# A halved first slab, slab splits between the angles, a staggered odd layer and shorter waits in the state steps of a two-block network on one core

## The reference

```
for l in range(DEPTH):
    hn = rms_norm(h, attn_norm[l])
    proj = hn @ w_in[l]
    ...
def rope(x, positions):
    inv = ROPE_BASE ** (-jnp.arange(0, d, 2, dtype=jnp.float32) / d)
    ang = positions.astype(jnp.float32)[..., None] * inv
    cos, sin = jnp.cos(ang), jnp.sin(ang)
...
def step(state, inp):                      # RWKV-7, done in chunks of 64 tokens
    sa = jnp.einsum('bhvk,bhk->bhv', state, -kkt)
    state = (state * wt[:, :, None, :] + sa[..., None] * (kkt * at)[:, :, None, :]
             + vt[..., None] * kt[:, :, None, :])
...
def odd_layer(x, norm_pre, ...):
    h = rmsnorm(x, norm_pre)
    proj = h @ w_in                        # q, k, v, r, lr
```

## Time and profile before

| | |
|---|---|
| median of 3 runs | 2118.84 us (2118.39 to 2123.34) |
| profiled execution | 2119.92 us, span 2118.1 us |
| PE busy | 2010.8 us, 95% |
| DVE busy | 1124.9 us, 53% |
| ACT busy | 824.2 us, 39% |
| POOL busy | 92.5 us, 4% |
| first matmul | 14.10 us |

### The profile page before, as it was taken

The page is one execution under the profiler, slowest core; times in us unless marked ns, Lnnn a source line. Parts: engine busy times, 40 slices in busy tenths (PEclk is TensorE's granted clock), DMA queues, the critical chain, the costliest instruction groups (busy, mean ns, idle before and its releaser), DMA issues.

```text
span 2118.1 us, 29241 instructions
## 1 busy us (share of the span) xinstructions
PE 2010.8 (95%) x12552; PEld 1616.5 (76%) x12552; DVE 1124.9 (53%) x1566; ACT 824.2 (39%) x1160; POOL 92.5 (4%) x61
## 2 busy tenths in 40 slices
PE   6998799999999999888899999999999999889997
PEld 4875487888888887647688888887778777679886
DVE  7456755543344545567554434447667673543373
ACT  4246533322222323664332222235464653324362
POOL 4010120000000000103000000000000000100000
PEclk9999999999999999989999999999999999999999
DMA  5310011222322322100032232223222222222111
GB/s 210 110 60 23 2 43 60 100 87 82 119 100 69 121 90 82 40 1 23 27 108 90 86 121 88 86 95 119 100 80 99 81 80 99 80 71 79 60 51 40
DMA packets 26192, 167.35 MB, mean 79 GB/s; under 512 B 2896, under 2 KB 3152, under 8 KB 10192
## 3 DMA queue, kind: packets, MB, share of 16 engines
q1 hardware_dynamic: 26064, 165.48, 22.4%
HBM read 163.38 MB, written 2.10 MB: 78 GB/s over the span
## 4 chain that ended last, share of the span: by engine, by line
PE 87%; DVE 9%; ACT 3%; issue 1%; DMA 0%; DVEq 0%; SPq 0%; ACTq 0%
PE bank L670 25%; PE bank L671 24%; PE bank L672 24%; PE bank L696 5%; PE bank L901 3%; DVE ring_low L1920 2%; ACT ring_high L1397 1%; PE bank L802 1%; DVE bank L2155 1%; PE bank L915 1%; DVE arena L2168 1%; PE bank L1268 1%; PE bank L1287 1%; DVE arena L2219 1%; PE bank L889 0%
## 5 line engine op out<-in xcount | busy, mean ns | idle before, releaser
L670 PE MATMUL bank<-arena_split,ring_high 128*128 128x512 f32 x2188 | 869.3, 397 | 48.6 <-DVE ring_low L1920 37.1
L671 PE MATMUL bank<-arena_split,ring_high 128*128 128x512 f32 x2188 | 857.7, 392 | 0.0
L672 PE MATMUL bank<-arena_split,ring_low 128*128 128x512 f32 x2188 | 857.2, 392 | 0.0
L670 PEld LDWEIGHTS bank<-arena_split,ring_high 128*128 128x128 f32 x2188 | 414.6, 190 | 149.2 <-DVE ring_low L1920 27.5
L671 PEld LDWEIGHTS bank<-arena_split,ring_high 128*128 128x128 f32 x2188 | 414.6, 189 | 89.1 <-issue 4.5
L672 PEld LDWEIGHTS bank<-arena_split,ring_low 128*128 128x128 f32 x2188 | 414.3, 189 | 87.2
L1920 DVE TENSOR_TENSOR ring_low<-ring,ring_high 128x2048 fp32r<-128x2048 f32 (+3 forms) x161 | 344.4, 2140 | 176.6 <-ACT ring_high L1397 176.0
L1397 ACT ACTIVATE ring_high<-ring 128x2048 fp32r<-128x2048 f32 (+3 forms) x161 | 284.6, 1769 | 382.6 <-PE bank L672 379.8
L1415 ACT ACTIVATE arena<-bank 128x512 f32<-128x512 f32 x72 | 43.1, 598 | 291.5 <-DVE bank L1901 291.5
L1901 DVE TENSOR_TENSOR bank<-bank,rstd 128x512 f32<-128x512 f32 x72 | 50.3, 698 | 121.5 <-PE bank L672 121.5
L1366 ACT ACTIVATE arena<-bank 128x512 f32<-128x512 f32 (+1 forms) x73 | 42.3, 594 | 137.5 <-PE bank L672 62.6
(11 more groups left out here) (343 smaller groups left out, 1829.2 us busy)
## 6 DMA issues: line engine op xcount, KB each, us to landing
ring<-slabs_in SPq DMA_DIRECT2D x122, 1024.0 KB, 4.8
ring<-slabs_in SPq DMA_DIRECT2D x32, 704.0 KB, 4.1
con<-con_in SPq DMA_DIRECT2D x1, 2208.0 KB, 12.0
h<-x_in SPq DMA_DIRECT2D x4, 512.0 KB, 9.1
out<-arena SPq DMA_DIRECT2D x8, 256.0 KB, 2.0
ring<-slabs_in SPq DMA_DIRECT2D x3, 512.0 KB, 3.4
ring<-slabs_in SPq DMA_DIRECT2D x2, 768.0 KB, 4.4
arena<-gates_in SPq DMA_DIRECT2D x1, 1536.0 KB, 9.8
```

Of the source, the lines that this page charges most:

```text
L670: pe.matmul(out, weight[0], right[0], start=start, stop=False)
L671: pe.matmul(out, weight[0], right[1], start=False, stop=False)
L672: return pe.matmul(out, weight[1], right[0], start=False, stop=stop)
```

## The change

Six edits, all to the order of work and its waits. The arithmetic stays.

First, the slab `in0_r` comes in two transfers of half its columns, the transfers of x between them, and each half is split by itself; PE's first group waits for the first half alone. ACT loads its table at once, and POOL starts its squares when the first slab is split. Second, the split of `in0_v` goes into the middle of the first angle, and the split of `in0_lo_mq0` behind the angles; the norm's sum moves from the middle of `in0_k` into the middle of `in0_v`. Third, in the odd layer each tile's step has three products, two for `qk` 0 and 1 and one for 2 or 3; the other eight follow when all tiles are there, and `slab_group` of `odd_qk0` names group `qk` 1. The splits of `odd_qk2` and `odd_qk3` stand ahead of the norm's root on ACT and DVE, the norm's sum stands between `qk` 4 and 5, and POOL waits for all eight squares. Fourth, the copies that signalled `transition_ready` and `state_ready` go; PE waits for the addition itself. Fifth, on DVE `in0_mq12` is split behind two evictions of banks instead of six. Sixth, the squares of the last head are summed one product step earlier.

```
@@ tensor engine
             def norm_sum(tag):
+                pe.wait_ge(ones_loaded, 16)
                 pe.wait_ge(squares_summed, cnt.next(squares_summed))
...
-                pe.wait_ge(transition_ready, cnt.next(transition_ready))
+                for n in range(2):
+                    pe.wait_ge(*taken(("G", l, n)))
                 for c in range(1, NC - 1):
...
-                    pe.wait_ge(state_ready, cnt.next(state_ready))
                     bk = group(("st", l, c), "dve")
+                    if c == 1:
+                        pe.wait_ge(state_ready, cnt.next(state_ready))
+                    else:
+                        pe.wait_ge(*taken(("st", l, c - 1)))
...
-                pe.wait_ge(state_ready, cnt.next(state_ready))
+                pe.wait_ge(*taken(("st", l, NC - 2)))
...
-                pair(f"in{l}_r", [("pa", l, 0), ("pa", l, 1)], ["dve"] * 2, parts_step, (lambda: norm_sum(("attn", l))) if l else None)
-                pair(f"in{l}_k", [("pa", l, 2), ("pa", l, 3)], ["dve"] * 2, None, None if l else (lambda: norm_sum(("attn", l))))
-                pair(f"in{l}_v", [("pa", l, 4), ("pa", l, 5)], ["dve"] * 2)
+                if l:
+                    pair(f"in{l}_r", [("pa", l, 0), ("pa", l, 1)], ["dve"] * 2, parts_step, lambda: norm_sum(("attn", l)))
+                else:
+                    first = ring_high[:, 0, :], ring_low[:, 0, :]
+                    pe.wait_ge(first_half_split, 1)
+                    split_gemm(("pa", l, 0), "dve", split_tiles(first, 0, DT), hn_parts, parts_step)
+                    split_gemm(("pa", l, 1), "dve", split_tiles(split_slab(f"in{l}_r"), DT * P, DT), hn_parts)
+                pair(f"in{l}_k", [("pa", l, 2), ("pa", l, 3)], ["dve"] * 2)
+                pair(f"in{l}_v", [("pa", l, 4), ("pa", l, 5)], ["dve"] * 2, None, None if l else (lambda: norm_sum(("attn", l))))
...
+            later = [(n, k) for k in range(DT) for n in (2, 3)]
             for k in range(DT):
                 parts_step(k)
-                for n, (bk, w) in enumerate(held):
-                    mm = product(bk[:, :], w[k], hn_parts[k], k == 0, k == DT - 1)
-                    if k == DT - 1:
-                        mm.then_inc(psum_ready, 1)
+                for n in range(2):
+                    odd_product(n, k)
+                odd_product(*later.pop(0))
+            for n, k in later:
+                odd_product(n, k)
             for n in range(2):
-                slab_group[slab_index[f"odd_qk{n}"]] = len(order) - 1
...
+                slab_group[slab_index[f"odd_qk{n}"]] = book["qk", 2 * n + 1][0]
...
+            pair("odd_qk2", [("qk", 4), ("qk", 5)], ["dve"] * 2, None, odd_norm_sum)
+            pair("odd_qk3", [("qk", 6), ("qk", 7)], ["dve"] * 2)
...
-                    if n == 0 and k == 1:
+                    if n == 0 and k == 0:
                         gla_squares(3, last_squares)
@@ scalar engine
+            act.preload_act_table_set(ROOTS)
             act.wait_ge(epsilon_ready, cnt.next(epsilon_ready, 5))
...
                         if m == 1:
-                            prepare(f"in{l}_r", 1)
+                            act.wait_ge(first_half_loaded, 16)
+                            f(ring_high[:, 0, FIRST_HALF], ring[:, 0, FIRST_HALF], ACT.Copy).then_inc(cnt.up(first_half_high), 1)
+                    act.wait_ge(slab_loaded[0], 16)
+                    f(ring_high[:, 0, SECOND_HALF], ring[:, 0, SECOND_HALF], ACT.Copy).then_inc(cnt.up(slab_high_ready), 1)
...
                 if l == 0:
+                    prepare(f"in{l}_k")
...
-                    prepare(f"in{l}_k")
+                    prepare(f"in{l}_v")
...
+            prepare("odd_qk2")
             inverse_root(("ss", "odd"), rstd[:, :], D)
-            for m in range(4):
-                prepare(f"odd_qk{m}")
+            prepare("odd_qk3")
@@ vector engine
                         ts(turns, turns, MAGIC, None, SUB).then_inc(cnt.up(dve_done), 1)
-                        dve.wait_ge(cnt.sem, cnt.value)
+                        turned_down = cnt.value
+                        if n == 0:
+                            prepare(f"in{l}_k")
+                        dve.wait_ge(dve_done, turned_down)
...
-                    prepare(f"in{l}_k")
+                    prepare(f"in{l}_v")
...
+                    if m == 2 and l == 0:
+                        prepare(f"in{l}_lo_mq0")
...
                        ADD).then_inc(cnt.up(dve_released), 1)
-                    dve.wait_ge(cnt.sem, cnt.value)
-                    cp(stat[:, 0, 0:1], stat[:, 1, 0:1]).then_inc(cnt.up(state_ready), 1)
...
             post_norm("even_post", "even_post", residual_ready, lambda m: f"even_out{m}", 16, "odd_pre")
+            prepare("odd_qk2")
@@ gpsimd
+            pool.wait_ge(slab_split, 1)
...
+            pool.wait_ge(residual_square_ready, DT)
             for m in range(DT):
-                pool.wait_ge(residual_square_ready, m + 1)
@@ sync
-                sp.dma_start(ring[:, n % SLOTS, 0:cols], src).then_inc(slab_loaded[n % SLOTS], 16)
+                if n == 0:
+                    sp.dma_start(ring[:, 0, FIRST_HALF], src[:, FIRST_HALF]).then_inc(first_half_loaded, 16)
+                    for m in range(1, 4):
+                        sp.dma_start(h[:, 2 * m:2 * m + 2, :], x_in[:, 2 * m:2 * m + 2, :]).then_inc(x_loaded[m], 16)
+                    sp.dma_start(ring[:, 0, SECOND_HALF], src[:, SECOND_HALF]).then_inc(slab_loaded[0], 16)
```

More of the change, by code:

```diff
@@ L403, in A @@
             return arena[:, t:t + n, :]
+        FIRST_HALF = slice(0, DT * P)
+        SECOND_HALF = slice(DT * P, 2 * DT * P)
         def R(t):
@@ L427, in two_blocks @@
         slab_high_ready, slab_split = sem("slab_high_ready"), sem("slab_split")
+        first_half_loaded = sem("first_half_loaded")
+        first_half_high, first_half_split = sem("first_half_high"), sem("first_half_split")
         high_ready, parts_ready = sem("high_ready"), sem("parts_ready")
@@ L473, in two_blocks @@
         end_diagonal_ready = sem("end_diagonal_ready")
-        transition_ready = sem("transition_ready")
         state_ready = sem("state_ready")
@@ L1170, in _, with odd_product, odd_norm_sum @@
                 held.append((group(("qk", n), "dve"), w))
+            def odd_product(n, k):
+                bk, w = held[n]
+                mm = product(bk[:, :], w[k], hn_parts[k], k == 0, k == DT - 1)
+                if k == DT - 1:
+                    mm.then_inc(psum_ready, 1)
+            later = [(n, k) for k in range(DT) for n in (2, 3)]
             for k in range(DT):
                 parts_step(k)
-                for n, (bk, w) in enumerate(held):
-                    mm = product(bk[:, :], w[k], hn_parts[k], k == 0, k == DT - 1)
-                    if k == DT - 1:
-                        mm.then_inc(psum_ready, 1)
-            for n in range(2):
-                slab_group[slab_index[f"odd_qk{n}"]] = len(order) - 1
-            pe.wait_ge(odd_squares_summed, 1)
-            gemm(("ss", "odd"), "act", rows, [cst("ones")], [A(8)[:, 0, :]])
-            for n in range(2, 4):
-                pair(f"odd_qk{n}", [("qk", 2 * n), ("qk", 2 * n + 1)], ["dve"] * 2)
+                for n in range(2):
[3 more added lines that the diff above has]
+                odd_product(n, k)
+            for n in range(2):
+                slab_group[slab_index[f"odd_qk{n}"]] = book["qk", 2 * n + 1][0]
+            def odd_norm_sum():
+                pe.wait_ge(odd_squares_summed, 1)
+                gemm(("ss", "odd"), "act", rows, [cst("ones")], [A(8)[:, 0, :]])
+            pair("odd_qk2", [("qk", 4), ("qk", 5)], ["dve"] * 2, None, odd_norm_sum)
+            pair("odd_qk3", [("qk", 6), ("qk", 7)], ["dve"] * 2)
             split_gemm("lr", "dve", split_tiles(split_slab("odd_lr"), 0, DT), hn_parts)
@@ L1425, in _ @@
                         if m == 1:
-                            prepare(f"in{l}_r", 1)
+                            act.wait_ge(first_half_loaded, 16)
+                            f(ring_high[:, 0, FIRST_HALF], ring[:, 0, FIRST_HALF], ACT.Copy).then_inc(cnt.up(first_half_high), 1)
+                    act.wait_ge(slab_loaded[0], 16)
+                    f(ring_high[:, 0, SECOND_HALF], ring[:, 0, SECOND_HALF], ACT.Copy).then_inc(cnt.up(slab_high_ready), 1)
+                    splits.append(f"in{l}_r")
                 prepare(f"in{l}_r")
                 if l == 0:
+                    prepare(f"in{l}_k")
                     for n in range(2):
@@ L2020, in _ @@
                         if m == 1:
-                            prepare(f"in{l}_r", 1)
+                            dve.wait_ge(first_half_high, 1)
+                            tt(ring_low[:, 0, FIRST_HALF], ring[:, 0, FIRST_HALF], ring_high[:, 0, FIRST_HALF].bitcast(F32),
+                               SUB).then_inc(cnt.up(first_half_split), 1)
+                    dve.wait_ge(slab_high_ready, cnt.next(slab_high_ready))
```

(10 more changed lines are left out.)

3 lines of the change are left out of this document (removed).

## The result

The changed kernel takes **2103.1 us** (median of four executions, 2097.12 to 2103.99) against 2118.61 of the kernel before beside it (2113.44 to 2123.34). The ratio is 0.9913, with a 95% interval of 0.989 to 0.9935. The forecast was 2103.0.

The account below looks back on a forecast made before the run. PE, busy 95% of the span, was taken as the bound, so only its starts, waits and low clock counted. 7.0 + 7.7 + 1.1 = 15.8 us off 2118.84 gave 2103.0; range 2097 to 2110.

Parts of the forecast that it names:

- Start and angles: Layer 0 start and angle chain: earlier first matmul, no wait before `in0_v`, DVE and POOL taking turns; gain 7.0 us.
- the wait 2.6: Ahead of `in0_lo_mq0`: PE, done with `in0_v` at 46.2, waits 2.6 us for the slab, ready at 48.7.
- the low clock behind it: After the wait for `in0_lo_mq0`, PE runs at the lower clock again; charged 1.5 us, gain 8.5 without it.
- the wait of 0.7 at the norm sum: Inside `in0_v`: PE's norm sum waits for POOL's squares from 39.0 to 39.7, about 0.7 us.
- Odd layer: Start of the odd layer: earlier split of `odd_qk2` removes 5.6 us of wait and 2.1 of low clock, gain 7.7 us.
- one turn lost to POOL: Split of `odd_qk2`: DVE shut out once by POOL makes the slab ready at 1864.2 instead of 1863.1, needed at 1864.4.
- State steps: State steps: dropped copies save 0.19 us at each of six waits, 1.1 us; bounds 0.4 and 2.3.
- The sum: Whole kernel: 7.0 + 7.7 + 1.1 = 15.8 us gained, giving a median of 2103.0 us; chance 0.50.
- (a): Angle chain does not bind, DVE and POOL turns being kinder: gain 20.5 us, 2098.3; chance 0.20.
- (b): Start gives less: half slab lands near 9.5, POOL's squares end at 44.4; total gain 12.3 us, 2106.5; chance 0.18.
- (c): Odd layer: slab `odd_qk0` freed only with the last group, little wait saved; total gain 9.6 us, 2109.2; chance 0.09.
- (d): Slower: POOL's sum of squares holds PE in the middle of `in0_v`; 2129 if it comes at 70; chance 0.01.

Follow-up runs that it names:

- second candidate: Changed kernel with `in0_lo_mq0` split between the sines and `in0_mkv` also split earlier on ACT and DVE; 2098.04 us, ratio 0.9901 to the kernel before.
- first comparison: Whole change against the kernel before, four executions of the changed kernel: 2103.1 us against 2118.61, ratio 0.9913.
- second comparison: The same changed kernel timed again beside the kernel before: median 2100.46 us against 2119.85, ratio 0.9907.
- first candidate: Changed kernel with the `in0_lo_mq0` split moved earlier, between the sines and into the second angle; 2105.14 us, ratio 0.9945 to the kernel before.

## Why the prediction was right

**Start and angles, 7.0 forecast.** 6.6 at mark A between the means, 7.2 between the two profiles that the forecast compares. The steps came as walked through: first matmul 9.6 (9.76), `in0_k` low 21.4 (21.28), `in0_v` low 29.7 (29.56), the clip 35.8 (35.59), POOL's last addition 39.7 (39.34), angles done 42.6 (42.27), `in0_lo_mq0` ready 48.7 (48.47), the wait 2.6 (2.47), the low clock behind it 1.5 (nine matmuls in 3.38 us, so 1.3 lost). Wrong in small: the wait of 0.7 at the norm sum is not there, as POOL was done 0.2 us before PE came, and PE began with 12 slow matmuls, not 10, a number that scatters. (24 matmuls at the prediction's 0.229 us are 5.50, not 5.45; the trace's 0.227 gives 5.45.) What the prediction did not say, and the kernel with the whole slab showed: of the two edits the halved slab has no value of its own here. Whether it gains once the later waits are gone, as in the second candidate, was not tried.

**Odd layer, 7.7 forecast.** 7.4 by the odd stages of all profiles (8.0 by the first five), 6.4 us (3.8 to 8.9) by the timing. `odd_qk2` was ready 22.4 us behind the stage's first matmul and needed at 23.1; the forecast had 22.4 to 23.5, the latter with one turn lost to POOL, and 23.7. So the cover is 0.7 us; a second turn lost, 1.1 us by the prediction's rows, would by this sum have brought a wait back. The lows came 1.93 us apart (1827.13, 1829.06, 1830.98).

**State steps, 1.1 forecast.** 0.9 by the second layer's trace, doubled. Its timing, 3.0 us with an interval that reaches from -0.2 to 5.9, cannot tell it from nothing. The first waiting step starts 0.15 us behind the addition, not 0.06. In the second layer the 0.19 a time holds where the wait fell from 0.58 to 0.38 and nearly at the readout (0.66 to 0.49), but at the other waiting step the wait of the weight load fell only from 0.42 to 0.36. So the term was a little too large, and six equal savings of 0.19 are not what happened.

**The sum, 15.8.** 6.6 + 7.4 + 0.9 = 14.9 by the traces (15.5 with 8.0 for the odd layer), 15.5 between the medians of the first comparison; 18.4 (13.8 to 23.3) and 19.7 (15.7 to 23.7) by the two ratios. The two profiled executions differ by 22.8, and 7 us of that have nothing to do with the change, as the next section shows. That 2103.1 was measured where 2103.0 was forecast is luck to this digit: four executions of the changed kernel went from 2097.12 to 2103.99, and the second comparison lies 1 to 4 us lower. Rivals (a) to (d) are out: the wait before `in0_lo_mq0` is there, the half slab came at 7.40, ACT got the slab with the first two groups, and POOL was done at 39.34.

## What to carry to other kernels

An earlier start of the bound engine is worth only what the next late buffer lets through: before a start is polished, follow the chain that sets the second and third wait. Moving a split forward can move the wait to a later slab: with `in0_lo_mq0` alone moved nothing was gained at mark A, with `in0_mkv` moved too 3.8 us. (`in0_mkv` alone was not tried.) And a helper engine that slows another, as POOL does DVE here, is best placed where the other has nothing that is waited for, even if it then ends late itself.

## What the runs showed of the hardware

**Identical code takes 864 to 873 us.** From mark A to the odd layer the changed kernel, the one with the whole slab and the first candidate run the same instructions. Windows from 155 us to the second state readout, in the changed kernel, the whole slab's, and the candidate's profile:

```profile
155.00:1019.00 864.00, 818.77 (x6901) 643.96 (x6900) 462.52 (x779) 332.70 (x525) 50.94 (x32) 0.98 0.19 65
```

```profile
155.00:1021.00 866.00, 821.52 (x6901) 645.64 (x6900) 462.34 (x778) 332.92 (x525) 50.91 (x32) 0.98 0.19 64
```

```profile
155.00:1028.00 873.00, 825.73 (x6901) 644.91 (x6899) 464.49 (x778) 332.54 (x525) 52.10 (x32) 0.97 0.18 64
```

The same 6901 matmuls keep PE busy 7 us longer; the granted clock is a hundredth lower. The stretches at the lower level behind short waits fall differently from one execution to the next: the 56 matmuls of the first state readout take 1.85 us in the changed kernel and 2.72 in the one with the whole slab. Counted from the end of the wait at mark A to the second readout, nine profiles of the same code take 871.3 to 880.6 us. The kernel before shows it over its 23 executions of the second comparison: 2108.59 us at a mean clock of 0.986, 2124.18 at 0.977. That is why differences of a few us are read from the marks here, and even the 7 to 8 us between the first candidate and the changed kernel, timed in different comparisons, are not laid to the edit. Whether the change also makes such stretches rarer (its mean clock in the second comparison is 0.983, that of the kernel before 0.981) is open; it would explain the 3 to 5 us by which the ratios exceed the sum. It was only argued, not tried, and the eight kernels timed later speak against it: their gains by the ratios, each brought to the changed kernel by the difference at its two marks, estimate the whole change at 13.0 to 18.7 us, 15.2 in the mean.

**Slow matmuls at a clock of 1.00.** The first 12 matmuls, from 9.76 on, come 0.43 us apart as in the low stretches, but the window's granted clock reads 1.00. Their number goes from 7 (one square on POOL) to 13 (the second candidate) over the profiles here, in no order that I can tie to an edit.
